# Expert blocks of a mixture-of-experts step: another order of products and turns on TensorE, and other permits for the weight loads

## What is computed

```python
def hier_moe(x, w_rg, b_rg, w_re, b_re, w_eg, w_eu, w_ed):
    ...
    combine = jnp.sum(jax.nn.one_hot(eid, N_EXPERTS, dtype=jnp.float32) * gate[..., None], axis=1)
    hg = jnp.einsum('nd,edf->nef', x, w_eg)
    hu = jnp.einsum('nd,edf->nef', x, w_eu)
    hidden = jax.nn.silu(hg) * hu * combine[..., None].astype(x.dtype)
    return jnp.einsum('nef,efd->nd', hidden, w_ed)
```

## Time and profile before

| what | value |
|---|---|
| median of 3 runs | 1457.71 us (1456.45 to 1466.41) |
| profiled execution, span from first to last instruction | 1455.5 us |
| mean granted TensorE clock | 0.936 of full speed |
| PE busy | 1293.9 us, 89% of the span |
| DVE, ACT, POOL busy | 711.7, 447.8, 498.3 us |
| line 1416, up products | 1568 records, 192.1 us busy |
| line 1440, down products | 392 records, 98.1 us busy |
| lines 1398 and 1426, turns | 49 x 4 and 49 transposes |

### The profile page before, as it was taken

One profiled execution on the slowest core, in us unless ns is written; L12 is line 12 of the kernel. 1 busy time (PEld: TensorE's weight loads), 2 busy tenths in 40 slices (PEclk: granted clock), 3 DMA queues, 4 the chain that ended last, 5 costly groups with the idle time before them and its releaser, 6 DMA issues.

```text
span 1455.5 us, 19176 instructions
## 1 busy us (share of the span) xinstructions
PE 1293.9 (89%) x7452; PEld 811.2 (56%) x7452; DVE 711.7 (49%) x1362; ACT 447.8 (31%) x932; POOL 498.3 (34%) x455
## 2 busy tenths in 40 slices
PE   5699999896798667998999999998979899999986
PEld 5624777675563333554566647886855454555442
DVE  2409999999998993333410022434432222222215
ACT  1550134353234368544543321222111111111110
POOL 1300086879644412443533310000023343444420
PEclk9899999998898766999999997999889999999998
DMA  7601212122444413555746452028029999999945
GB/s 265 230 13 58 62 58 81 46 79 91 132 150 160 167 55 111 186 186 164 225 129 196 161 207 95 29 95 342 27 86 416 388 416 419 373 406 419 410 169 197
DMA packets 86873, 272.95 MB, mean 188 GB/s; under 512 B 16280, under 2 KB 48744, under 8 KB 75832
## 3 DMA queue, kind: packets, MB, share of 16 engines
q1 hardware_dynamic: 49776, 157.25, 28.2%
q0 software_dynamic: 34528, 111.21, 22.6%
q10 hardware_dynamic: 2479, 3.27, 0.7%
HBM read 292.55 MB, written 22.98 MB: 217 GB/s over the span
## 4 chain that ended last, share of the span: by engine, by line
PE 53%; DVE 26%; DMA 12%; issue 3%; ACT 3%; POOL 2%; ACTq 0%; SPq 0%; POOLq 0%; DVEq 0%
PE ps L1416 9%; PE ps L1076 6%; DVE arena L1852 5%; DVE arena L1851 5%; DVE arena L1853 5%; PE ps L1440 5%; PE ps L1082 5%; PE ps L1265 5%; PE ps L1273 4%; DMA arena<-in_cache_kv,arena 3%; DMA arena<-scr_x,arena 3%; PE ps L1116 3%; PE ps L1134 2%; DMA arena<-in_w_dn,arena 2%; PE ps L1152 2%
## 5 line engine op out<-in xcount | busy, mean ns | idle before, releaser
L1076 PE MATMUL ps<-arena 128*128 128x288 f32 (+4 forms) x1216 | 315.9, 425 | 3.9 <-ACT arena L1642 3.3
L1076 PEld LDWEIGHTS ps<-arena 128*128 128x128 f32 (+1 forms) x1216 | 228.6, 200 | 88.1 <-issue 31.1
L1416 PE MATMUL ps<-arena 128*64 128x256 f32 x1568 | 192.1, 388 | 4.3 <-DMA arena<-in_w_gu 2.0
L982 POOL DMA_INDIRECT arena<-in_cache_kv,arena x128 | 127.1, 993 | 158.5 <-PE ps L1134 121.7
L1416 PEld LDWEIGHTS ps<-arena 128*64 128x64 f32 x1568 | 110.0, 139 | 83.6 <-issue 28.7
L1514 ACT ACTIVATE arena<-ps 128x256 f32<-128x256 f32 (+6 forms) x144 | 59.1, 419 | 217.9 <-PE ps L1265 60.6
L1025 POOL DMA_INDIRECT arena<-scr_x,arena x49 | 49.7, 1014 | 184.9 <-DVE arena L2221 170.3
L1032 POOL DMA_INDIRECT scr_ypair<-arena x49 | 50.4, 1029 | 181.2 <-ACT arena L1784 174.1
L954 POOL TENSOR_TENSOR arena<-arena 128x816 f32<-128x816 f32 x58 | 103.0, 1775 | 17.2 <-ACT arena L1532 10.4
L1440 PE MATMUL ps<-arena 128*64 128x512 f32 x392 | 98.1, 623 | 11.5 <-DMA arena<-in_w_dn,arena 11.5
L1082 PE MATMUL ps<-arena 128*128 128x256 f32 (+4 forms) x544 | 106.4, 359 | 1.8 <-ACT arena L1648 1.2
(11 more groups left out here) (335 smaller groups left out, 1717.5 us busy)
## 6 DMA issues: line engine op xcount, KB each, us to landing
arena<-in_w_gu SPq DMA_DIRECT2D x32, 2048.0 KB, 12.8
arena<-in_w_dn SPq DMA_DIRECT2D x32, 1024.0 KB, 14.8
arena<-in_w_in SPq DMA_DIRECT2D x20, 1024.0 KB, 5.5
arena<-in_w_o SPq DMA_DIRECT2D x4, 1024.0 KB, 5.5
arena<-in_w_pg SPq DMA_DIRECT2D x4, 1024.0 KB, 9.0
arena<-scr_ypair SPq DMA_DIRECT2D x4, 1024.0 KB, 7.9
arena<-in_cache_kv,arena POOLq DMA_INDIRECT x192, 4.5
arena<-in_x_prompt SPq DMA_DIRECT2D x4, 512.0 KB, 8.0
```

What stands on the lines that cost most here:

```text
L982: pl.indirect_dma_start(unit_rows[:, 2 * j + t, half * H * HD:(half + 1) * H * HD], None, I["cache_kv"].rearrange("n (h d) -> (n h) d", h= ...
L1076: mm = nc.tensor.matmul(out, w[:, k], hT[:, k, a:b], start=(k == 0), stop=(k == KC - 1))
L1416: mm = nc.tensor.matmul(PS[2 + p % 2][64 * half:64 * half + 64, 0:2 * P], xT[:, p % 3, j, 64 * h:64 * h + 64], w[:, k, half, :], start=(k ...
```

## The change

On TensorE the up product of a block is one run without a turn inside it; the down product comes two blocks behind its up product and not one; the turn of the hidden rows of block p-1 and the x turn, now of block p+2 and no longer of p+1, stand side by side. ACT and DVE follow the new order: ACT evicts block p-2 after the sigmoid of p, DVE makes the hidden rows of p first, then copies the turned ones of p-1 and p+2. On SP the gate and up weights of expert e wait for the up product of expert e-3, the down weights for its down product. POOL's list is unchanged.

```diff
             def load_expert(e):
                 s = e % 3
+                if e >= 3:
+                    sp.wait_ge(u_full, POS[("base", e - 3)] + 1)
                 sp.dma_start(eset[s][:, 0:2 * KC * F], I["w_gu"][e * P:(e + 1) * P, :]).then_inc(up_in[s], 16)
+                if e >= 3:
+                    sp.wait_ge(y_full, POS[("base", e - 3)] + 1)
                 sp.dma_start(eset[s][:, 2 * KC * F:], I["w_dn"][e * P:(e + 1) * P, :]).then_inc(down_in[s], 16)
...
             for e in range(3, NE):
-                sp.wait_ge(y_full, POS[("base", e - 3)] + 1)
                 load_expert(e)
...
             turn(0)
+            turn(1)
             for p in range(NBLK):
-                up_half(p, 0)
+                up(p)
+                if p >= 2:
+                    down(p - 2)
                 if p:
                     hid_turn(p - 1)
-                up_half(p, 1)
-                if p + 1 < NBLK:
-                    turn(p + 1)
-                if p:
-                    down(p - 1)
+                if p + 2 < NBLK:
+                    turn(p + 2)
+            down(NBLK - 2)
             hid_turn(NBLK - 1)
             down(NBLK - 1)
...
             for p in range(NBLK):
                 sigmoid_act(p)
-                if p:
-                    rows_act(p - 1)
+                if p >= 2:
+                    rows_act(p - 2)
+            rows_act(NBLK - 2)
             rows_act(NBLK - 1)
...
             xt_dve(0)
+            xt_dve(1)
             for p in range(NBLK):
+                hid_dve(p)
                 if p:
                     ht_dve(p - 1)
-                if p + 1 < NBLK:
-                    xt_dve(p + 1)
-                hid_dve(p)
+                if p + 2 < NBLK:
+                    xt_dve(p + 2)
```

More of the change, by code:

```diff
@@ L1399, in turn, with up @@
                 mm.then_inc(xt_full, 1)
-            def up_half(p, part):
+            def up(p):
                 kind, n = BLOCKS[p]
@@ L1404, in up_half @@
                 w = up_weights(eset[n % 3]) if kind == "base" else over_up[k % 2]
-                if part == 0:
-                    if kind == "base":
-                        pe.wait_ge(up_in[n % 3], 16 * (n // 3 + 1))
-                    else:
-                        pe.wait_ge(over_up_in[k % 2], 16 * (k // 2 + 1))
-                    pe.wait_ge(xt_drained, p + 1)
-                    if p >= 2:
-                        pe.wait_ge(hid_ready, p - 1)
-                for k in range(4 * part, 4 * part + 4):
+                if kind == "base":
+                    pe.wait_ge(up_in[n % 3], 16 * (n // 3 + 1))
+                else:
+                    pe.wait_ge(over_up_in[k % 2], 16 * (k // 2 + 1))
+                pe.wait_ge(xt_drained, p + 1)
+                if p >= 2:
+                    pe.wait_ge(hid_ready, p - 1)
+                for k in range(KC):
                     h, j = divmod(k, 4)
@@ L1418, in up_half @@
                                               start=(k == 0), stop=(k == KC - 1))
-                if part == 1:
-                    mm.then_inc(u_full, 1)
+                mm.then_inc(u_full, 1)
             def hid_turn(p):
```

## The result

| | before | after |
|---|---|---|
| median of the runs, us | 1458.68 (1456.45 to 1466.41, 4 runs) | 1484.26 (1483.64 to 1489.64, 4 runs) |
| ratio after / before, 95% interval | | 1.0177 [1.0146, 1.0209] |
| span of the profiled execution, us | 1455.5 | 1482.6 (the execution's own time 1484.42) |
| expert stage: first up to end of last down | 1083.02 to 1415.77: 332.7 | 1078.89 to 1442.51: 363.6 |

The changed kernel is slower by 1.8%. The stage grew by 30.9 us. In the profiled execution what lies ahead of it was 4.1 us shorter (that start varies between 1078.9 and 1084.5 us among kernels whose code is the same up to there), so that the span grew by 27.1 us. Lines of after: up 1418, down 1441, hid turn 1427, x turn 1401, gather 1028, scatter 1035, loads of over weights 1013 (up) and 1020 (down), SP's loads 817 and 820.

The account below looks back on a forecast made before the run. PE was taken to set the pace, with DMA engines only just following and gather landing time the hidden resource. Terms -14 - 15 + 40 + 11 + 8 = +30 us gave a median of 1488 us, range 1462 to 1526.

Parts of the forecast that it names:

- Seams, -14: On PE, gaps between operand shapes shrink: 0.30 us a block over 47 blocks, -14 us; block 6.02 us.
- Weight loads, -15: PE's 12.0 us of weight waits and a 2.7 us half-clock stretch go: -15 us at best, 0 if they stay.
- Gathers, +40: x turns wait for gathers: 12 behind two loads land in near 10.0 us with 6.7 left, 3.3 us each, +40.
- the bound from below: Shortest gather landing, 3.4 us, taken as reached where both over loads ahead of it had nothing to fetch.
- Clock, +11: PE runs at half clock after stops: 0.9 us for each of 12 stops, +11 us (0 to 32).
- End, +8: Last blocks: PE stops 6.8 us at up(48) for its over load, further work follows; +8 us (5 to 13).
- Start, 0: First blocks cost nothing; two turns take 0.6 us more ahead of up(0), down(0) is deferred by the same work.
- The signs: Profile after: x turn waits 25 us or more, 6.0 us block, longest stop at up(48) or down(48), idler DMA, clock falls.
- The first (gathers suffice): Gathers land within 6.7 us behind loads, so no x turn stops; faster, 1437 us; chance 7%.
- The second (the DMA engines bound it): Full DMA engines make weights late for a faster PE; no change, 1457 to 1471, say 1464 us; chance 13%.
- The third (the ring as slow as the queues): Gathers land in 12.3 us, +67, with more half clock and end; 1541 us, half way 1515; chance 18%.
- The fourth (late w_dn of base experts): PE waits at down for later base down weights, not for gathers; 1477 us; chance 5%.

Follow-up runs that it names:

- permits_only: The kernel before with only the changed kernel's new waits for SP's weight loads, engine orders old; ratio 1.0081 to before, median 1472.39 us.
- lead1: The changed kernel with each gather issued one block earlier in POOL's list; ratio 1.0099 to before, median 1476.16 us.
- lead2: The changed kernel with each gather issued two blocks earlier in POOL's list; ratio 1.0077 to before, median 1472.82 us.

## Why the prediction was right

The forecast was 1488 us; the median is 1484.3. Its terms, against the profile. Between the start of up(3) and that of up(46), 43 blocks, before took 1391.09 - 1103.43 = 287.7 us and after 1404.34 - 1100.56 = 303.8: +16.1. That is -12.9 for the seams, -14.7 for before's waits and its stretch at the lower clock, which are gone, +31.5 for turn waits, +9.4 for turns and up products at the lower clock behind them, and a rest of +2.8. Most of the rest, some 2.2 us by estimate, lies in the 14 stops themselves: the view counts each from the modelled end of the turn ahead of it, 0.33 us after its start, where in an undisturbed block the next starts 0.17 us after it. From up(46) to the end it is +13.5, of which 1.8 is a down product that now lies behind up(46); from up(0) to up(3) it is +1.3, or +3.1 with that product counted. Together the stage grew by 30.9 us, where the sum said 30.

That the total is so close is luck in part: gathers and clock came out 10.1 us below their terms, the end, the start and the rest 9.6 us above theirs. The span grew by 27.1 us, as what lies ahead of the stage was shorter in the profiled execution, and the median by 25.6.

**Seams, -14.** The sum is right to the hundredth: 6.02 us a block. Its parts are off by up to 0.06 us either way (up 3.50, down 1.82, hid turn 0.17, x turn 0.53). The extra wait between the two kinds of turn costs nothing.

**Weight loads, -15.** The waits for SP's weights are gone. That one step, "an earlier request brings nothing but a place in a queue", was right in bytes and wrong in effect: permits_only shows a price of 0.8% in the old order.

**Gathers, +40.** The mechanism, the place and the window were right (lead1 and lead2 show it); the term measured 31.5. Its count was off. I took 12 gathers behind two loads at 3.3 us each. Six stops of 2.2 to 7.2 us make 26.2 of the 31.5, mean 4.4, and eight of at most 1.3 the rest. The packets of POOL's queue tell why: a row of w_gu is a packet of 16,384 bytes, and from 1110 to 1400 us such packets appear in five bursts of 128 only (1166, 1208, 1289, 1332 and 1375 us). The other over up loads had nothing to fetch. Five of the six stops follow one of these bursts; the sixth is the stop at 1133.03, behind a full down load and an up load with nothing to fetch. I should have counted loads that move data in the trace of before, instead of loads. The landing was off as well: the term took 10.0 us for all. Five gathers behind a full up load landed in 9.8 to 13.2 us, eight behind one with nothing to fetch in 3.0 to 7.1, and gather(8) in 15.6. So there were fewer stops than were summed, and longer ones, and the two errors partly cancel. And the 3.4 us of the earlier trace rows, the bound from below, is the gather issued at 1259.12 us, which had nothing to fetch itself. POOL's queue (software_dynamic) moved no data from 1258.7 to 1266 us in before (packets, MB, share):

```profile
q0 software_dynamic: 320, 0.00, 2.2%
```

**Clock, +11.** 9.4 measured, in five stretches. They follow stops of 2.23 to 7.22 us; the stop of 3.01 us cost nothing.

**End, +8.** Measured +12. From the start of down(44) to the end of down(48) it is 34.7 us, where I had 33.6 and before 27.2, so the step itself was 1.1 us short: up(48) ran nearly all at the lower level (6.60 us). The rest is the place of the step's start. Down(44) itself moved, which my sum from down(44) onwards left out: before it started 2.5 us ahead of up(46), after it starts 3.5 us behind it. Those 6.0 us, less the 1.8 of the product that is counted elsewhere, are the other 4.

**Start, 0.** Wrong, by +3. PE stopped for 3.85 us at up(2), which then ran at the lower level:

```profile
1080.85 0.99 POOL L1013 DMA_INDIRECT arena<-in_w_gu,arena  x1 [0.30 <-issue]
...
1083.23 0.34 SPq L817 DMA_DIRECT2D arena<-in_w_gu  x1
...
1091.93 6.28 PE L1418 MATMUL ps<-arena 128*64 128x256 f32 x32 [3.85 <-DMA arena<-in_w_gu,arena]
```

The load issued at 1080.85 took 11.0 us, where before's took 8.5. SP's first w_gu went out at 1083.23, right behind up(0), as the new permit allows, and shares the engines with it; before it came at 1097.32.

**The signs.** The x turn waits, the undisturbed period, the DMA slices and the clock are as foretold. One sign failed: the longest stop is not at up(48) (6.38 us) or down(48) but at the x turn of block 8 (7.22).

**The rivals.** The first (gathers suffice) is out. The second (the DMA engines bound it) is out as the cause of the result, as they idled for 48.4 us of the stage instead of 21.7 (their busy time is 315.2 us, before 311.1). It may still hold for what can be won: busy for 311 of 333 us, they leave little. That each cure moved the wait on doesn't show it, as the engines had idle time in those stages (0.89 busy in lead2). The third (the ring as slow as the queues) is out: median landing 9.9 us. The fourth (late w_dn of base experts) is out; down waited once, for an over load.

## What to carry to other kernels

An engine's list in order passes a delay on to everything behind it. Who moves a consumer later must look at what stands behind its release in every queue, and move the independent requests (gathers, loads) ahead of it in the same edit: here the reordering cost 1.8% by itself, and with its gathers and loads moved and one more buffer the kernel was 0.8% faster than before. A shorter block of PE is no gain by itself: the old order with nearly the same help had as short a stage (320.7 beside 320.3 us). Where transfers nearly fill the DMA engines, a cure is read from what the next wait is, not from the wait that is gone; the same early permit was worth 1.0% in the new order (1.0284 over 1.0177) and cost 0.8% in the old one.

## What the runs showed of the hardware that was not expected

A load whose indices all lie out of bounds moves nothing and keeps its place in the ring: it lands behind what is ahead of it. These are three landings of after: the over up load issued at 1116.07 us, with full queues and no packet of 16,384 bytes in POOL's queue; the full down load issued at 1144.27; and the up load with nothing to fetch behind it, issued at 1145.60.

```profile
DMA to landing us min/median/max: 14.4/14.4/14.4
...
DMA to landing us min/median/max: 5.5/5.5/5.5
...
DMA to landing us min/median/max: 4.4/4.4/4.4
```

The third landed at 1150.0, 0.2 us behind the down load ahead of it (1149.8). Of the nine such up loads issued between 1100 and 1400 us eight landed within 0.2 us of the down load ahead. The ninth is the first of these lines: its down load, issued at 1114.74, took 11.7 us and landed at 1126.4, and it landed 4.1 us later, at 1130.5; why, the trace doesn't show. So the 4.4 us from issue to landing is not what such a load costs those behind it. It is mostly the wait for what stands ahead.

The clock after a stop does not follow from the stop's length alone. These are two x turns of after with the up products behind them:

```profile
1177.35 0.66 PE L1401 MATMUL ps<-arena 128*128 128x128 f32 x4 [3.01 <-DMA arena<-scr_x,arena]
1177.93 3.67 PE L1418 MATMUL ps<-arena 128*64 128x256 f32 x32
...
1384.20 1.11 PE L1401 MATMUL ps<-arena 128*128 128x128 f32 x4 [2.23 <-DMA arena<-scr_x,arena]
1385.24 4.71 PE L1418 MATMUL ps<-arena 128*64 128x256 f32 x32
```

After 3.01 us the engine ran on at full speed (3.67 us), after 2.23 us the turns and part of the up product ran at the lower level (1.11 and 4.71 us). What decides it these runs don't show. A cost for the clock can only be given as a mean over stops, as here: 9.4 us over the six turn stops of more than 2 us.
